# Moving the early parts of an output product inside a chain of two attentions

## What is computed

```python
x = x + 0.5 * swiglu_half(x, ...)          # ffn before
h = rms_norm(x, mix_norm[layer])
z = h @ ab_w_in[e]
o_a = mla_mixer(z[..., :AB_MLA_COLS], ...)      # 8 heads of 64 values, causal softmax
o_b = dilated_mixer(z[..., AB_MLA_COLS:], ...)  # 12 heads of 64 in 3 groups of 4, softmax over the 3 groups together
mixed = jnp.concatenate([o_a, o_b], axis=-1) @ ab_w_out[e]   # 256 x 768 by 768 x 1024
x = x + mixed
x = x + 0.5 * swiglu_half(x, ...)          # ffn after
```

## Time and profile before

| | us |
|---|---|
| median of three runs | 1713.15 |
| profiled execution | 1711.66 |
| its span | 1709.9 |
| PE busy in the span | 1634.5 |
| DVE busy | 1132.4 |
| ACT busy | 937.7 |
| POOL busy | 119.0 |

### The profile page before, as it was taken

The page is one execution under the profiler, slowest core; times in us unless marked ns, Lnnn a source line. Parts: engine busy times, 40 slices in busy tenths (PEclk is TensorE's granted clock), DMA queues, the critical chain, the costliest instruction groups (busy, mean ns, idle before and its releaser), DMA issues.

```text
span 1709.9 us, 24655 instructions
## 1 busy us (share of the span) xinstructions
PE 1634.5 (96%) x8997; PEld 1376.9 (81%) x8997; DVE 1132.4 (66%) x1808; ACT 937.7 (55%) x1520; POOL 119.0 (7%) x172
## 2 busy tenths in 40 slices
PE   8998999989899998999999799999999998899999
PEld 7886888888678886888887578888888887578887
DVE  5955765677675567766667466667666673667665
ACT  5554655557565555555566565556555554665554
POOL 0601000000000000000003300000000010410000
PEclk9999999999999998999999999999999997999999
DMA  9332464574345644656464045565555573026652
GB/s 318 124 123 99 148 199 169 203 251 135 108 144 176 218 150 148 199 170 212 173 242 148 1 140 189 187 198 171 181 187 194 199 250 124 1 79 217 199 169 99
DMA packets 216786, 283.91 MB, mean 166 GB/s; under 512 B 8328, under 2 KB 152712, under 8 KB 216712
## 3 DMA queue, kind: packets, MB, share of 16 engines
q1 hardware_dynamic: 216712, 282.93, 49.5%
HBM read 281.81 MB, written 1.09 MB: 165 GB/s over the span
## 4 chain that ended last, share of the span: by engine, by line
PE 85%; DVE 8%; ACT 4%; issue 1%; SPq 1%; POOL 0%; DMA 0%; ACTq 0%; DVEq 0%
PE banks L966 29%; PE banks L967 15%; PE banks L739 12%; PE banks L740 11%; PE banks L741 11%; DVE ring_lo L348 1%; PE banks L1288 1%; PE banks L1321 1%; PE banks L1301 1%; ACT ring_hi L340 1%; PE banks L1651 1%; SPq L446 1%; DVE stats L580 1%; PE banks L2910 1%; PE banks L670 1%
## 5 line engine op out<-in xcount | busy, mean ns | idle before, releaser
L966 PE MATMUL banks<-act_both,ring_hi 128*128 128x512 f32 x2112 | 751.2, 397 | 3.3 <-DVE act_both L612 1.6
L967 PE MATMUL banks<-act_both,ring_lo 128*128 128x256 f32 x2112 | 592.4, 281 | 0.0
L966 PEld LDWEIGHTS banks<-act_both,ring_hi 128*128 128x128 f32 x2112 | 397.3, 188 | 100.4 <-issue 4.4
L967 PEld LDWEIGHTS banks<-act_both,ring_lo 128*128 128x128 f32 x2112 | 397.4, 188 | 5.0
L1082 DVE TENSOR_TENSOR ring_lo<-weight_slots,ring_hi 128x1024 fp32r<-128x1024 f32 x240 | 283.3, 1222 | 62.5 <-ACT ring_hi L1037 62.2
L348 DVE TENSOR_TENSOR ring_lo<-weight_slots,ring_hi 128x1024 fp32r<-128x1024 f32 (+4 forms) x150 | 182.0, 1226 | 98.1 <-ACT ring_hi L340 95.0
L1037 ACT ACTIVATE ring_hi<-weight_slots 128x1024 fp32r<-128x1024 f32 x240 | 239.2, 1044 | 1.1 <-DMA weight_slots<-in_ffn_w 1.1
L1051 ACT ACTIVATE normed<-banks 128x512 f32<-128x512 f32 x132 | 78.9, 597 | 289.4 <-PE banks L967 289.4
L739 PE MATMUL banks<-ffn_down_hi,ffn_hidden_hi 128*128 128x512 f32 x528 | 207.5, 393 | 0.4
L740 PE MATMUL banks<-ffn_down_lo,ffn_hidden_hi 128*128 128x512 f32 x528 | 206.8, 392 | 0.0
L741 PE MATMUL banks<-ffn_down_hi,ffn_hidden_lo 128*128 128x512 f32 x528 | 205.8, 390 | 0.0
(11 more groups left out here) (372 smaller groups left out, 1916.2 us busy)
## 6 DMA issues: line engine op xcount, KB each, us to landing
weight_slots<-in_ffn_w SPq DMA_DIRECT2D x44, 1024.0 KB, 6.5
weight_slots<-in_ffn_w_gate SPq DMA_DIRECT2D x44, 1024.0 KB, 5.4
weight_slots<-in_ffn_w_up SPq DMA_DIRECT2D x44, 1024.0 KB, 8.0
weight_slots<-in_ffn_w_down SPq DMA_DIRECT2D x88, 512.0 KB, 8.4
weight_slots<-in_ffn_w SPq DMA_DIRECT2D x44, 512.0 KB, 8.3
weight_slots<-in_ev_w_in SPq DMA_DIRECT2D x6, 2048.0 KB, 12.2
weight_slots<-in_od_w_in SPq DMA_DIRECT2D x5, 2048.0 KB, 11.4
weight_slots<-in_ab_w_in SPq DMA_DIRECT2D x4, 2048.0 KB, 11.3
```

The source lines that it names most:

```text
L966: pe.matmul(bank, k.hi(n)[:, q, :], k.act_both[:, q], start=q == 0, stop=False, skip_group_check=True)
L967: return pe.matmul(bank[:, 0:S], k.lo(n)[:, q, :], k.act_hi[:, q, :], start=False, stop=q == KD - 1, skip_group_check=True)
```

## The change

The parts table and the split table of the third layer's `attend` are replaced. Parts 0 to 3 were taken one by one in steps 6, 8, 10 and 12. They are now taken two by two in steps 6 and 8, and steps 10 and 12 have none. The splits of parts 4 and 5 move from the end of step 11 and of step 13 both to the end of step 9, those of parts 6 and 7 from the end of step 15 to that of step 13.

```diff
-        attend(k, block, Chain(mla, dil, 4), out, {6: [0], 8: [1], 10: [2], 12: [3]}, {1: 3, 3: 4, 11: 5, 13: 6, 15: 8},
+        attend(k, block, Chain(mla, dil, 4), out, {6: [0, 1], 8: [2, 3]}, {1: 3, 3: 4, 9: 6, 13: 8},
                side=ab, tile_waits=tile_waits)
```

## The result

The changed kernel takes 1725.54 us (median of three, 1723.90 to 1727.14), 12.4 us more than 1713.15. The ratio is 1.0063 [1.0043, 1.0083]. Measured a second time, beside new runs of the kernel before on one chip, it is 1.0059 [1.0043, 1.0075], about 10 us. The forecast was 1720.4, with a range up to 1726: slower, as said, and by more than said. It is inside the range by 0.5 us, and the highest of the three runs is outside.

A forecast was written before the change was run, and what follows sets the result against it. TensorE was taken as the bound, with 85% of the chain, so only filling or opening its waits counts. Terms 5.7 - 2.0 + 2.2 + 1.4 = +7.3 us gave a median of 1720.4 us, range 1716.5 to 1726.

The forecast's parts named there:

- More parts ahead of the last scores: Steps 6 to 8: two more parts ahead of the last scores delay them and the second exponentials, +5.7 us.
- Part 2 gone from step 10: Step 10: part 2 lay beside the exponentials, where PE waited for ACT anyway; removing it gains nothing, 0.
- The splits: End of step 9: splits of parts 4 and 5 stand ahead of the copy PE waits for, ACT 1.9, DVE 0.3, +2.2 us.
- Part 3's room: Step 12: without part 3 the way between two groups of transposes shortens, if POOL keeps up, -2.0 us.
- Loads and splits of parts 6 and 7: Splits at the end of step 13 fit before ACT's next copy, and loads have over 20 us to spare: 0.
- The clock: Transposes and values behind the second exponentials run slow after a 5.7 us idle of PE, at half clock: +1.4 us.
- rival 1: TensorE's clock stays at full rate in this stage: +5.9 us, 1719.0 us; chance 0.20.
- Outside the stage: The stage runs from part 0's first matmul in step 6 to the last parts' first; no cost forecast elsewhere.
- rival 3: The clock stays low through the sparse later steps: about +12 us, +18 at worst, 1725 to 1731 us; chance 0.13.
- rival 2: The splits at the end of step 9 cost nothing, only the parts count: +3.7 us, 1716.8 us; chance 0.08.
- rival 4: Step 9's transposes wait for POOL, so early parts cost nothing: +0.2 us (1713.4) or -2.0 us (1711.2); chance 0.07.

The follow-up runs named there:

- one early: The kernel before with part 1 alone moved from step 8 to step 6; ratio to the kernel before 1.0012 [1.0000, 1.0023].
- Both split kernels: The changed kernel with all splits placed as in the kernel before (ratio 1.0040), or with the splits of parts 4 and 5 at the end of step 8 (1.0026).
- Denser: The changed kernel with thrown-away matmuls in all waits of PE behind the last scores (steps 10 to 14); ratio to the kernel before 1.0021.
- both in 10: The kernel before with part 3 moved from step 12 to step 10, beside part 2; ratio 0.9987 [0.9971, 1.0002].
- spread: The kernel before with part 3 cut up: half at the end of step 10, the rest in waits of steps 11 and 12; ratio 0.9971.
- The filled kernel: The changed kernel with 18 thrown-away matmuls at the end of step 10, in PE's long wait; ratio to the kernel before 1.0044.
- dense: The changed kernel with 18 thrown-away matmuls at the end of step 10 and three in each of steps 11 to 14; ratio to the kernel before 1.0035.

## Why the prediction was right, and where not

**More parts ahead of the last scores, +5.7.** Measured +5.61. The working holds, also that POOL would be ready first. What it made too little of is that part 1's place in step 8 was itself beside POOL's scaling; one early shows this at 2.64 us. In the sum it didn't matter, since parts 2 and 3 filled the same place.

**Part 2 gone from step 10, 0.** The wait grew from 1.57 to 5.53, and nothing was won.

**The splits, +2.2.** Measured 1.88 on ACT and 0.4 on DVE, 2.3. Both split kernels take the 1.9 away.

**Part 3's room, -2.0.** Hidden in the first trace (-0.57, as the slow clock stands against it). Denser shows it at full clock, 2.54 us in place of 4.50. That POOL keeps up held there, but not in both in 10 and spread, where 1.67 and 1.66 are left.

**Loads and splits of parts 6 and 7, 0.** The way from the transposes of unit 5 to the last parts is 4.29 in both, and from there to the norm's transposes 5.73 in both (993.11 to 998.84, 1006.95 to 1012.68), so 0.

**The clock, +1.4.** This is the term that was mis-sized. What is left in the table after the others is 1.79 - 0.4 = 1.4, then -0.57 + 2.0 = 1.4, then 0.42: 3.2 us in the first trace, and more in the second, whose slow stretch was 17 us and whose stage was 42.5. I let the clock come back 4 us after PE's restart, as in rows 8 and 9; it took 9 us. Without it the sum stands: 5.6 - 2.0 + 2.3 = 5.9, as rival 1 had it, and denser, at full clock, comes to 37.8 - 31.4 = 6.4 with its fillers.

**Outside the stage, 0.** The median moved by 12.4 and the forecast by 7.3. Of the 5.1 between them the clock has 1.8. Against the other 3.3 the traces have only the shift outside the stage (4.71 less 1.3), nearly all of it ahead of everything that was changed, and the kernel before shows shifts as large against itself. That the median still came out inside the range, by 0.5 us, is in part luck. Against the new runs of the kernel before the change costs about 10 us.

So the mechanism held, and the measured stage is 1.8 us beyond the forecast, on the side of rival 3. Rival 3's reason was the right one, though not its price: the thin steps, not only the wait, keep the clock low. The Trainium skill ("TensorE: Matmul & The Clock Gate", section "A second HAM failure mode: psum-queue depth-cycling") tells of a kernel in which frequent small idles between groups of matmuls made the clock go to and fro. The filled kernel agrees: its long wait was gone and the clock fell in steps with waits of 1.50 us at most. But the page doesn't say which thin steps: both in 10 has the same waits of 0.74 from step 11 on and kept 1.00. Rival 1 fell by the windows, rival 2 by ACT's row, rival 4 by POOL's.

## What to carry to other kernels

A wait on one engine is a place for work only if that work stands inside it in the engine's own list; moved ahead of the instruction that starts the other engine's chain, the same work is paid in full, and the wait grows by most of it. So fill behind what the chain starts with, in pieces no longer than the waits. Splits and copies at the end of a step are cheap only if nobody waits for the next instruction of that engine.

## What was not expected of the hardware

TensorE's clock stood at half rate for 7 to 20 us in this stage (7, 14, 14, 17 and 20 us in five traces with parts 0 to 3 in steps 6 and 8), though PE was at work again within 5 us. In dense only 3.4 us of it were left and in denser none. Once slow, the transposes take 0.87 in place of 0.52 and values 1.55 in place of 0.87. What brings the clock back was not settled, nor why it was low in steps 4 to 6 of some executions and not of others.
